# Transposes of the second attention's probabilities on row halves, and constant products in three idle times

## The reference, cut to what matters

```python
def hybrid_layer(x, c, ...):                       # 512 tokens, 1024 wide
    h = rms_norm(x, norm_gain) * (1 + scale) + shift
    proj = h @ w_in                                # q, k, v, z of both branches
    o_a = banded_gqa(qa, ka, v_a, SWA_WINDOW, rel_bias[:, :A_HEADS], sinks)   # 8 heads, 128 back
    k_cmp = qk_norm(compress_blocks(kc, ...)); v_cmp = compress_blocks(vc, ...)   # 31 blocks
    o_cmp, o_sel = nsa_cmp_sel(qb, k_cmp, v_cmp, k_sel, v_sel, bias_b)
    o_win = banded_gqa(qb, k_win, v_win, NSA_WINDOW, bias_b, None)
    o_b = gb[0] * o_cmp + gb[1] * o_sel + gb[2] * o_win
    y = concat([o_a * silu(z_a), o_b * silu(z_b)])
    return x + gate * (y @ w_out)
...
    logits_c = einsum('btgrd,bngd->bgrtn', qi, kc)       # compressed scores
    p_c = masked_softmax(logits_c, c_end <= t)
    o_cmp = einsum('bgrtn,bngd->btgrd', p_c, vc)
```

## Time and profile before

| | us |
|---|---|
| median of 3 runs | 1581.78 |
| lowest and highest | 1579.65, 1583.51 |
| profiled execution, device time | 1581.26 |
| its span, first to last instruction | 1579.6 |

### The profile page before, as it was taken

One profiled execution on the slowest core, in us unless ns is written; L12 is line 12 of the kernel. 1 busy time (PEld: TensorE's weight loads), 2 busy tenths in 40 slices (PEclk: granted clock), 3 DMA queues, 4 the chain that ended last, 5 costly groups with the idle time before them and its releaser, 6 DMA issues.

```text
span 1579.6 us, 29878 instructions
## 1 busy us (share of the span) xinstructions
PE 1545.8 (98%) x12549; PEld 1354.1 (86%) x12549; DVE 898.9 (57%) x1368; ACT 542.9 (34%) x835; POOL 98.1 (6%) x106
## 2 busy tenths in 40 slices
PE   9999999999999989989999999999999999999998
PEld 8999999999998679978888888888888787777787
DVE  6655245565479787555445655534555554367862
ACT  6222122222245562024223322222232243247860
POOL 0000000000001460000000000000000000001310
PEclk9999999999999999999999999999999999999999
DMA  7343334354432200002233222132222343211001
GB/s 283 143 148 104 108 107 149 121 128 121 127 88 81 62 2 31 5 15 80 83 112 111 95 92 94 67 118 107 90 88 92 105 190 134 80 40 55 2 5 77
DMA packets 27666, 147.68 MB, mean 93 GB/s; under 512 B 2928, under 2 KB 3328, under 8 KB 16944
## 3 DMA queue, kind: packets, MB, share of 16 engines
q1 hardware_dynamic: 21616, 122.50, 22.3%
q0 software_dynamic: 5424, 22.68, 5.2%
q10 hardware_dynamic: 528, 1.08, 0.2%
HBM read 140.97 MB, written 5.27 MB: 93 GB/s over the span
## 4 chain that ended last, share of the span: by engine, by line
PE 89%; DVE 6%; DMA 1%; issue 1%; ACT 1%; POOL 1%; SPq 0%; DVEq 0%; ACTq 0%
PE PS L644 24%; PE PS L645 24%; PE PS L646 24%; PE PS L997 2%; PE PS L1007 2%; PE PS L1032 2%; PE PS L1097 1%; PE PS L1082 1%; PE PS L1095 1%; PE PS L912 1%; DMA SILUC<-in_c 1%; DVE WLO L1836 1%; PE PS L1307 1%; DMA H<-in_h 1%; DVE TAB L2023 1%
## 5 line engine op out<-in xcount | busy, mean ns | idle before, releaser
L644 PE MATMUL PS<-UH,WHI 128*128 128x264 f32 (+1 forms) x1088 | 327.2, 301 | 3.1 <-DVE WLO L1836 3.1
L645 PE MATMUL PS<-UH,WLO 128*128 128x264 f32 (+1 forms) x1088 | 325.7, 299 | 0.0
L646 PE MATMUL PS<-UL,WHI 128*128 128x264 f32 (+1 forms) x1088 | 325.4, 299 | 0.0
L1354 ACT ACTIVATE WHI<-RAW 128x2048 fp32r<-128x2048 f32 (+3 forms) x124 | 210.4, 1696 | 313.2 <-PE PS L646 305.2
L1836 DVE TENSOR_TENSOR WLO<-RAW,WHI 128x2048 fp32r<-128x2048 f32 (+3 forms) x124 | 251.2, 2026 | 77.5 <-ACT WHI L1354 76.8
L644 PEld LDWEIGHTS PS<-UH,WHI 128*128 128x128 f32 x1088 | 204.9, 188 | 10.1 <-DVE WLO L1836 2.6
L645 PEld LDWEIGHTS PS<-UH,WLO 128*128 128x128 f32 x1088 | 204.8, 188 | 6.5 <-issue 0.2
L646 PEld LDWEIGHTS PS<-UL,WHI 128*128 128x128 f32 x1088 | 204.5, 188 | 6.3
L644 PE MATMUL PS<-UHS,WHI 128*128 128x512 f32 x520 | 206.3, 397 | 0.0
L645 PE MATMUL PS<-UHS,WLO 128*128 128x512 f32 x520 | 203.6, 391 | 0.0
L646 PE MATMUL PS<-ULS,WHI 128*128 128x512 f32 x520 | 203.5, 391 | 0.0
(11 more groups left out here) (427 smaller groups left out, 2684.9 us busy)
## 6 DMA issues: line engine op xcount, KB each, us to landing
RAW<-in_f2u SPq DMA_DIRECT2D x22, 1024.0 KB, 4.8
RAW<-in_f1u SPq DMA_DIRECT2D x21, 1024.0 KB, 4.8
ADA<-in_ada POOLq DMA_DIRECT2D x24, 512.0 KB, 4.6
RAW<-in_f1d SPq DMA_DIRECT2D x16, 704.0 KB, 4.0
RAW<-in_f2d SPq DMA_DIRECT2D x16, 704.0 KB, 4.1
RAW<-in_wi SPq DMA_DIRECT2D x10, 1024.0 KB, 4.8
RAW<-in_w SPq DMA_DIRECT2D x8, 1024.0 KB, 4.8
RAW<-in_mg SPq DMA_DIRECT2D x8, 1024.0 KB, 4.8
```

Of the source, the lines that this page charges most:

```text
L644: mm(out, WHI[:, slot, c:c + w], hi, start=first, stop=False)
L645: mm(out, WLO[:, slot, c:c + w], hi, start=False, stop=False)
L646: return mm(out, WHI[:, slot, c:c + w], lo, start=False, stop=last)
L1354: A(WHI[:, slot, 0:w], RAW[:, slot, 0:w], ACT.Copy).then_inc(hi_rdy, 1)
```

## The change

Four edits. First, in the second attention a 128x128 transpose becomes two transposes of 64 queries: rows 0 to 63 of the probabilities go to bank 4, rows 64 to 127 to bank 5, and the two p lie one behind the other in a bank. Each copy (`turned`) now takes one half of the queries of both p, writes runs of 64 elements, and starts when all transposes of the step are done; PE waits for both copies ahead of the first transpose. What is computed and the layout of `PTS2` stay the same. ACT drops a wait for the transposes ahead of the exponentials; its copy, earlier in the same iteration, waits for the same count.

Second, `keep_busy(times)` multiplies constants of the table `TAB` into bank 7, 384 columns at a time, in three places: three products ahead of `square_sums(4)`, four ahead of `wv`, four in iteration 2 of the attention ahead of the wait for the exponentials. Nobody reads these results.

Third, `compressed_scores(qi)` does one query tile, and is called at k = 4, 5, 6 and 7 of chunk 6.

```diff
@@ -473,6 +473,12 @@
         return out

     STEPS = pair_steps()
+
+    def turned(half, i, w):
+
+        src = PS[:, 4 + half, 0:w].rearrange("k (p t q) -> k p t q", p=2, q=CH)
+        dst = PTS2[:, i % 2, :, 0:w].rearrange("k p (t c q) -> k p t c q", c=2, q=CH)[:, :, :, half, :]
+        return dst, src
     LATENT = [dict(g=g, qi=QT - 1 - g, j=j, w=P * (QT - g), n=N_META + P * (QT - g), last=j == 3)
               for g in range(QT) for j in range(4)]
     WIDE = sum(x["n"] > SEQ for x in LATENT)
@@ -645,6 +651,11 @@
             mm(out, WLO[:, slot, c:c + w], hi, start=False, stop=False)
             return mm(out, WHI[:, slot, c:c + w], lo, start=False, stop=last)

+        def keep_busy(times):
+
+            for _ in range(times):
+                mm(PS[:, 7, 0:3 * P], ONES, TAB[:, 0:3 * P], start=True, stop=True)
+
         def square_sums(v):
             c0, w = NORMS[v]
             if v in SUMMED:
@@ -983,6 +994,8 @@
             for i in range(n + 3):
                 if i < n:
                     x, s = STEPS[i], i % 2
+                    if i == 2:
+                        keep_busy(4)
                     if i >= 2:
                         pe.wait_ge(exp_rdy, U0 + 2 * STEPS[i - 2]["done"])
                     elif i == 1:
@@ -999,14 +1012,19 @@
                     last.then_inc(s_ps, 1)
                 if 0 <= i - 2 < n:
                     x, s = STEPS[i - 2], i % 2
+                    if i >= 3:
+                        pe.wait_ge(pt_rdy, I0 + i - 2)
+                        pe.wait_ge(pc_rdy1, I0 + i - 2)
+                    tiles_ = x["m"] * x["w"] // P
                     for p in range(2):
                         pe.wait_ge(exp_rdy, U0 + 2 * x["at"] + x["m"] * (p + 1))
-                        if i >= 3:
-                            pe.wait_ge((pt_rdy, pc_rdy1)[p], I0 + i - 2)
-                        for t in range(x["m"] * x["w"] // P):
-                            last = nc.tensor.transpose(PS[:, 4 + p, t * P:(t + 1) * P],
-                                                       PB2[:, s, p, t * P:(t + 1) * P], IDENT)
-                        last.then_inc(pt_ps, 1)
+                        for t in range(tiles_):
+                            for c in range(2):
+                                rows, o = slice(CH * c, CH * (c + 1)), (p * tiles_ + t) * CH
+                                last = nc.tensor.transpose(PS[:, 4 + c, o:o + CH], PB2[rows, s, p, t * P:(t + 1) * P],
+                                                           IDENT[rows, rows])
+                                if p == 1 and t == tiles_ - 1:
+                                    last.then_inc(pt_ps, 1)
                 if 0 <= i - 3 < n and STEPS[i - 3]["last"]:

                     g = STEPS[i - 3]["group"]
@@ -1188,9 +1206,11 @@

         stream(pe, "wo", outward(MH, ML))
         ffn(1, N_META, SEQ)
+        keep_busy(3)
         square_sums(4)
         pe.wait_ge(s4_rdy, KD + 1)
         mm(PS[:, 3, 0:SEQ], ONES, GF[:, 0, 0:SEQ], start=True, stop=True).then_inc(ss_done, 1)
+        keep_busy(4)

         n = START["wv"]
         pe.wait_ge(evac, n)
@@ -1240,16 +1260,17 @@
             pe.wait_ge(kc_sq, 1)
             mm(PS[:, 6, 0:NCMP], BONES, KSQ[:, 0:NCMP], start=True, stop=True).then_inc(kc_ss, 1)

-        def compressed_scores():
-            pe.wait_ge(kc_rdy, 1)
-            pe.wait_ge(n_n, 2)
-            for qi in range(QT):
-                for h in range(NH):
-                    rows = slice(CH * (h // 4), CH * (h // 4) + CH)
-                    c = NCMP * (4 * qi + h % 4)
-                    last = mm(PS[:, 6 + h // 4, c:c + NCMP], P2[rows, 2 + h % 4, P * qi:P * (qi + 1)],
-                              KCF[rows, 0:NCMP], start=True, stop=True)
-            last.then_inc(cs_ps, 1)
+        def compressed_scores(qi):
+            if qi == 0:
+                pe.wait_ge(kc_rdy, 1)
+                pe.wait_ge(n_n, 2)
+            for h in range(NH):
+                rows = slice(CH * (h // 4), CH * (h // 4) + CH)
+                c = NCMP * (4 * qi + h % 4)
+                last = mm(PS[:, 6 + h // 4, c:c + NCMP], P2[rows, 2 + h % 4, P * qi:P * (qi + 1)],
+                          KCF[rows, 0:NCMP], start=True, stop=True)
+            if qi == QT - 1:
+                last.then_inc(cs_ps, 1)

         def compressed_transposed(qi):
             pe.wait_ge(cs_n, 1)
@@ -1275,8 +1296,8 @@
         def inside(j, k):
             if (j, k) == (4, 4):
                 compressed()
-            elif (j, k) == (6, 4):
-                compressed_scores()
+            elif j == 6 and k >= 4:
+                compressed_scores(k - 4)
             elif (j, k) == (8, 3):
                 compressed_transposed(0)
             elif (j, k) in ((8, 6), (9, 1), (9, 4)):
@@ -1604,10 +1625,10 @@
             for i in range(n + 5):
                 if 0 <= i - 2 < n:
                     w = STEPS[i - 2]["m"] * STEPS[i - 2]["w"]
-                    act.wait_ge(pt_ps, U0 + 2 * (i - 2) + 1)
+                    act.wait_ge(pt_ps, U0 + 2 * (i - 2) + 2)
                     if i >= 4:
                         act.wait_ge(pv_done, I0 + i - 3)
-                    A(PTS2[:, i % 2, 0, 0:w], PS[:, 4, 0:w], ACT.Copy).then_inc(pt_rdy, 1)
+                    A(*turned(0, i, w), ACT.Copy).then_inc(pt_rdy, 1)
                 if 0 <= i - 3 < n and STEPS[i - 3]["last"]:
                     g = STEPS[i - 3]["group"]
                     act.wait_ge(den_ps, G0 + g + 1)
@@ -1622,8 +1643,6 @@
                 if i < n:
                     x, s = STEPS[i], i % 2
                     for p in range(2):
-                        if i >= 2:
-                            act.wait_ge(pt_ps, U0 + 2 * (i - 2) + p + 1)
                         act.wait_ge(max_rdy, U0 + 2 * x["at"] + x["m"] * (p + 1))
                         for e, y in enumerate(x["pairs"]):
                             c = NH * x["group"] + 2 * y["j"] + p
@@ -2323,7 +2342,7 @@
                     dve.wait_ge(pt_ps, U0 + 2 * (i - 2) + 2)
                     if i >= 4:
                         dve.wait_ge(pv_done, I0 + i - 3)
-                    V.tensor_copy(PTS2[:, i % 2, 1, 0:w], PS[:, 5, 0:w]).then_inc(pc_rdy1, 1)
+                    V.tensor_copy(*turned(1, i, w)).then_inc(pc_rdy1, 1)
                 if i == n + 4:

                     dve.wait_ge(ot_hi, G0 + 2 * QT)
```

## The result

The changed kernel takes 1573.89 us (median of 6 runs, 1572.54 to 1575.39) against 1581.62 (6 runs, 1578.68 to 1583.51): a ratio of 0.9946, 95% interval 0.9936 to 0.9955. It is faster, by 7.7 us where 10.7 were forecast; the time lies inside the range. The span of the profiled execution fell from 1579.6 to 1571.0 us, 8.6 less.

A forecast was written before the change was run, and what follows sets the result against it. PE, busy 98% of the span, was taken as the bound. Gains of 6.7 (transposes), 0.2 (attention start), 1.5 (seam) and 2.3 us (compressed scores) sum to 10.7, taking 1581.3 to 1570.6 us; range 1564 to 1578.

The forecast's parts named there:

- the seam: Around two sums ahead of `wv`: constant products hidden in PE's idle times, ten `wv` products at full clock, 1.5 us gained.
- the compressed scores: Four blocks: 3.4 us gained by full clock, less 1.1 us for entering and leaving blocks, net 2.3 us gained.
- transposes at 60 ns: In the attention: halves load no faster than scores do, transposes gain nothing, 1577.3 us in all; chance 0.17.
- transposes at 107 ns: In the attention: a half transpose keeps 107 ns or halves don't overlap, 16.4 us slower, 1597.7 us; chance 0.07.
- the clock falling in the seam or behind the scores: Clock falls elsewhere or as before: seam gives nothing, scores cost 1.1 us, 1575.5 us in all; chance 0.08.
- ACT and DVE take over: In the attention: both copies gate all transposes, half of the 6.7 us is lost, 1574 us in all; chance 0.11.
- the 60 ns an instruction: Compressed scores at full clock: all 64 instructions take 4.1 us in place of 5.23, 1.1 us gained.
- The transposes: In the attention: 432 half transposes at 35 ns take 15.1 us for 23.1; passages give 4.6 us, 1.9 comes back.
- The attention as a whole: Shorter transposes gain 6.7 us, limited by ACT and DVE stretch by stretch; constants at its start gain 0.2 us.
- The ends: Attention's last two groups of transposes, between value products, keep their passage: 0.3 us gained each, 0.8 with the first ones.
- The start: Start of the attention: four constant products hidden in 3.35 us of waiting, 0.2 us gained, bounds 0 and 1.7.
- The two-pair steps: Attention steps of two pairs, 28.70 us: PE would give 3.3, ACT is busy 27.70, so 1.0 us gained.

The follow-up runs named there:

- The last four kernels: Changed kernel plus alternating heads and earlier DVE copy: scores in four blocks 1570.62 us, two blocks 1570.03, two with factors on POOL 1569.72, one block 1569.72.

## Why the prediction was right, and where not

**The mechanism was right in the main.** PE was the bound at the seam, in the compressed scores and in most of the attention; at the attention's start it was not. Three rivals are out: transposes at 60 ns, transposes at 107 ns, the clock falling in the seam or behind the scores. The fourth, *ACT and DVE take over*, holds in part. The median lies on its time, 1574, and that is partly luck: it loses half of the attention's 6.7 us, but of the 2.4 us that the stretches fall short of their forecast 1.1 were lost in the attention and 1.4 in the compressed scores (the seam gave 0.05 more). The medians fall short by 3.0; the other 0.6 is less than their spread.

**The seam**: forecast 1.5, measured 1.55. Fillers priced by the earlier trace rows, cover read from the earlier trace rows, products from the earlier trace rows: all three held. The six filler instructions took 2.10 us for the 1.92 worked out, with the end of the last among it.

**The compressed scores**: forecast 2.3, measured 0.93. The clock was full, as forecast, and a block costs 0.34 us to enter and leave for the 0.37 I had. The term that was mis-sized is the 60 ns an instruction of the earlier trace rows. I took them as the price of any such instruction; they are the price in the middle of a long block, where loads of the two halves overlap. In a block of eight products, four on each half in turn, only the middle overlaps: 1.48 us for 1.13, four times over, which is the missing 1.4 us. That the split was needed for the clock, as I had it, is not shown: one block with alternating heads kept it too. The order of the heads was in the lines that I quoted, and the overlap of halves was my own argument for the transposes; I did not apply it to the scores.

**The transposes**: I took 35 ns between bounds of 30 and 60, and they take 31, next to the lower bound. The 0.17 us of a passage came off behind scores and came back ahead of denominators, as forecast. For PE alone this would have been 1.9 us more than the sum had (27 groups of sixteen, 0.49 us for 0.56).

The Trainium skill ("TensorE: Matmul & The Clock Gate", section on LDWEIGHTS) would have made it 53 ns by its rule, as an estimate. The trace doesn't agree: it has 31 ns.

**The attention as a whole**: forecast 6.9 with its start, measured 5.8. By stretch the gains were 1.6, 1.4, 0.5, 2.4 and 0.1 for the 1.0, 1.7, 0.7, 2.5 and 0.8 forecast, and the start gave -0.2 for 0.2. Three of these are right to 0.3 us. Two steps failed:
- *The ends.* I took the gain of the last two groups of transposes as PE's own, 0.3 us each, 0.8 with the first ones. The three groups behind the last scores did get 1.2 us shorter (0.49, 0.71 and 0.69 us for three times 1.02). But PE waits 0.86 us there for DVE's copy of the group before, and 0.21 us for the denominators' factors, which ACT spreads behind its own copy. I had named the new wait for both copies, and cost it in the steps of 384 alone. In all it is 3.2 us, of which 0.68 lie in the start. Moving DVE's copy earlier gave 1.6 us back, but none of it at the ends.
- *The start.* Four products and a window at 0.50 look like a gain, but the same window of before showed ACT and DVE busy all of it. My bound of 0 was the answer for the clock.

The two-pair steps gave more than I took (1.6 for 1.0). I had set the limit by ACT's 27.70 busy of 28.70 us, but the work that falls into a stretch moves with the change. Cut at the scores of steps 4 and 13, ACT was busy 28.75 of 29.76 us before and 27.95 of 28.19 after: its idle time went from 1.0 to 0.2 us, and 0.8 us less of its work falls into the stretch. When POOL took the factors from ACT, these steps gave another 1.25 us and those ahead of them 0.5, so ACT was indeed what held them.

**What is left.** The last four kernels lie at 1569.7 to 1570.6 us, ratios of 0.9919 to 0.9924 against 0.9946 of the changed one; among each other they can't be told apart. The one I would keep has alternating heads, the early copy and one block of scores: it drops the split, and leaves POOL's order as it is.

## What to carry to other kernels

Work on half of the array's rows gains most when neighbours in the order lie on different halves (here 5.8 us against 1.6); check that in each loop that touches halves, the old ones too. When an edit makes an engine wait for two producers where it waited for one, look where in each producer's iteration that result stands, and move it ahead of work that nobody waits for. An operation moved to an idle engine costs what is queued ahead of it there, and not its own duration alone.

## What the runs showed of the hardware that I had not expected

- A half transpose (64 rows, 64 moving columns, plain 32-bit) takes 31 ns when the halves alternate, and 56 to 64 on one half; a score's load of 64 rows by 128 columns takes 110 ns on one half and 58 when they alternate (3.69 us for 64).
- Going from one use of the array's row halves to another (scores to transposes) costs nothing; going between row halves, the whole array and column halves costs about 0.2 us. This is read from differences between groups (0.49 and 0.71 us, 0.44 and 0.59); a group behind a wait takes 0.7 us too.
- PE takes work of the other half ahead of what stands earlier, but only a few instructions of it: with one half first, sixteen transposes took 0.79 us, between the 0.49 of full overlap and 1.0 of none.
- POOL copies 128x512 plain values (from a source of 8 columns, spread) in 0.61 us by the profile's record, half of what an operation on two such tensors takes it (1.27), and less than ACT's 0.71.
- A stretch of 3.4 us at half clock in the delta rule comes and goes between executions of kernels that are the same there. The seam's first sum starts at 1260.7 to 1261.4 us in the six traces without one, at 1262.3 to 1263.2 in the six with one, and at 1262.5 and 1263.9 in the two with two: 1 to 2 us. A difference of that size in one profile is no evidence.
